# Turns and lag products of the state-space tiles earlier in layer 1's head periods, and their powers from coefficient tables

## What is computed

```python
def s5_mixer(u, lam_re, lam_im, log_step, b_re, b_im, c_re, c_im, d_skip, w_glu, b_glu):
    ...
    mag = jnp.exp(lr * dt)
    ab_r = mag * jnp.cos(li * dt)
    ab_i = mag * jnp.sin(li * dt)
    ...
    bb_r = fr[..., None] * br - fi[..., None] * bi
    bb_i = fr[..., None] * bi + fi[..., None] * br
    ...
    _, _, s_r, s_i = lax.associative_scan(_complex_linear_combine, (a_r, a_i, bu_r, bu_i), axis=1)
    y = (jnp.einsum('blgp,gcp->blgc', s_r, c_re.astype(f32))
         - jnp.einsum('blgp,gcp->blgc', s_i, c_im.astype(f32))
         + d_skip.astype(f32).reshape(SSM_GROUPS, SSM_GROUP) * ug)
```

## Time and profile before

| | us |
|---|---|
| median of 3 runs | 2592.64 (2587.49 to 2593.14) |
| the profiled execution | 2586.36 |
| its span | 2584.7 |
| layer 1's tiles on PE, first to last | 552.7 to 1022.4 |
| mean granted clock of PE over the span | 0.985 |
| busy: PE, DVE, ACT, POOL | 96%, 65%, 47%, 24% |

### The profile page before, as it was taken

How to read it: one execution, slowest core, us unless ns; L and a number is a source line. 1 busy time by engine, 2 the same in 40 slices (tenths; PEclk the granted TensorE clock), 3 DMA queues, 4 the chain that set the end, 5 groups by cost and what they waited for, 6 DMA issues and landing times.

```text
span 2584.7 us, 50520 instructions
## 1 busy us (share of the span) xinstructions
PE 2476.3 (96%) x18072; PEld 2348.0 (91%) x18072; DVE 1691.9 (65%) x2556; ACT 1220.9 (47%) x1819; POOL 628.6 (24%) x1047
## 2 busy tenths in 40 slices
PE   7999999989999999999988999999999999999999
PEld 7899999989899999998888999999888888888888
DVE  7876666567777777667777766565555555555555
ACT  5344544445555555555665434444544444444443
POOL 3300031358778886220010222011000000000000
PEclk9999999999999999999999999999999999999999
DMA  6655575555555555555454777565666676767764
GB/s 234 209 181 195 175 221 178 186 173 174 166 177 182 186 184 188 159 165 191 141 169 152 234 234 239 201 218 173 191 191 187 187 187 186 186 186 187 187 185 157
DMA packets 217449, 484.85 MB, mean 188 GB/s; under 512 B 22760, under 2 KB 120724, under 8 KB 217088
## 3 DMA queue, kind: packets, MB, share of 16 engines
q1 hardware_dynamic: 182912, 415.29, 52.6%
q0 software_dynamic: 13216, 37.93, 4.7%
q10 hardware_dynamic: 21216, 30.22, 3.6%
HBM read 455.00 MB, written 31.08 MB: 188 GB/s over the span
## 4 chain that ended last, share of the span: by engine, by line
PE 69%; DVE 15%; issue 7%; ACT 5%; POOL 2%; ACTq 1%; DVEq 0%; DMA 0%; POOLq 0%
PE z_ps L1987 12%; PE z_ps L1988 12%; PE z_ps L1989 12%; PE z_ps L2323 6%; PE z_ps L2324 6%; PE z_ps L2329 6%; DVE w_lo L1297 5%; ACT w_hi L717 2%; PE o_ps L2358 1%; PE o_ps L2357 1%; PE o_ps L2356 1%; PE v_ps L2357 1%; PE v_ps L2356 1%; PE p_ps L2357 1%; PE v_ps L2358 1%
## 5 line engine op out<-in xcount | busy, mean ns | idle before, releaser
L1297 DVE TENSOR_TENSOR w_lo<-w_raw,w_hi 128x1024 fp32r<-128x1024 f32 x520 | 634.8, 1249 | 335.4 <-ACT w_hi L717 333.1
L1987 PE MATMUL z_ps<-x_hi,w_hi 128*128 128x256 f32 x2816 | 822.1, 292 | 16.9 <-DVE w_lo L1290 14.4
L1988 PE MATMUL z_ps<-x_lo,w_hi 128*128 128x256 f32 x2816 | 805.3, 286 | 0.0
L1989 PE MATMUL z_ps<-x_hi,w_lo 128*128 128x256 f32 x2816 | 804.9, 286 | 0.0
L717 ACT ACTIVATE w_hi<-w_raw 128x1024 fp32r<-128x1024 f32 x520 | 533.1, 1051 | 262.5 <-PE z_ps L1989 216.5
L1987 PEld LDWEIGHTS z_ps<-x_hi,w_hi 128*128 128x128 f32 x2816 | 549.0, 195 | 26.9 <-issue 18.8
L1988 PEld LDWEIGHTS z_ps<-x_lo,w_hi 128*128 128x128 f32 x2816 | 549.3, 195 | 1.0
L1989 PEld LDWEIGHTS z_ps<-x_hi,w_lo 128*128 128x128 f32 x2816 | 548.9, 195 | 0.0
L1877 DVE TENSOR_TENSOR w_lo<-w_raw,w_hi 128x1024 fp32r<-128x1024 f32 x262 | 320.8, 1225 | 314.8 <-ACT w_hi L1141 314.7
L1141 ACT ACTIVATE w_hi<-w_raw 128x1024 fp32r<-128x1024 f32 x262 | 277.7, 1060 | 427.9 <-PE z_ps L2329 272.5
L2323 PE MATMUL z_ps<-w_hi,x_hi 128*128 128x512 f32 x704 | 275.1, 391 | 0.6 <-DVE res L1853 0.6
(11 more groups left out here) (382 smaller groups left out, 4131.5 us busy)
## 6 DMA issues: line engine op xcount, KB each, us to landing
w_raw<-in_w SPq DMA_DIRECT2D x704, 512.0 KB, 4.3
w_raw<-in_w SPq DMA_DIRECT2D x80, 384.0 KB, 4.8
res<-tab_d POOLq DMA_DIRECT2D x32, 384.0 KB, 4.5
w_raw<-in_w SPq DMA_DIRECT2D x80, 128.0 KB, 2.9
tab_d<-arena ACTq DMA_DIRECT2D x32, 256.0 KB, 2.1
tab_d<-arena POOLq DMA_DIRECT2D x32, 128.0 KB, 3.4
sg_d<-arena ACTq DMA_DIRECT2D x32, 128.0 KB, 4.6
arena<-sg_d POOLq DMA_DIRECT2D x16, 256.0 KB, 3.8
```

What stands on the lines that cost most here:

```text
L1297: dve.tensor_tensor(w_lo[:, n % RING, :], w_raw[:, n % RING, :], w_hi[:, n % RING, :].bitcast(F32), ALU.subtract).then_inc(w_lo_ready, 1)
L1987: pe.matmul(z, wh, hi[:, kt, :], start=(first and i == 0), stop=False)
L1988: pe.matmul(z, wh, lo[:, kt, :], start=False, stop=False)
L1989: m = pe.matmul(z, wl, hi[:, kt, :], start=False, stop=(last and i == len(kts) - 1))
```

## The change

- DVE's `tile` is split into `tile_turns` and `tile_lags`. The even tile's turns move ahead of `split_lo(p, 2)`, its lags to behind `split_lo(p, 3)`, ahead of the softmax's scaling. The odd tile's turns take the place where the even tile was, ahead of `split_lo(p, 4)`; its lags stay at the period's end. In head 0, with its norm, the even lags stand behind `split_lo(p, 2)`, and ACT's part of tile 0 moves from behind `split_hi(p, 3)` to behind `split_hi(p, 2)`.
- PE's tile asks for `e_ready` and `m_ready` up to tile `st - 2` instead of `st - 1`. The askings ahead of job 1 and job 3 stay.
- POOL makes tables of coefficients once (`coefficients`, in layer 0): the factor times powers 0 to 4 for C, powers 1 to 3 for B, for all 32 tiles. A tile is then twelve tensor_tensor instructions with broadcast operands, six of 160 columns and six of 96, no power waiting for the one before. The C half comes first and no longer waits for B. `load_c` for the next tile is issued after seven of them. A packed copy of the step times is made too.
- DVE waits once, at the start of layer 1, for the tables.

```diff
+                c_re, c_im, b_re, b_im = over(c_in[:, 0, :], 5), over(c_in[:, 1, :], 5), over(x[:, 0, 8, :], 3), over(x[:, 1, 8, :], 3)
+                c_out, b_out = [x[:, r, 0:5, :] for r in range(2)], [x[:, r, 5:8, :] for r in range(2)]
+                pool.tensor_tensor(c_tmp, c_im, by(c_coef, 1, 5), ALU.mult).then_inc(xt_step, 1)
+                pool.tensor_tensor(c_out[0], c_re, by(c_coef, 0, 5), ALU.mult).then_inc(xt_step, 1)
+                pool.tensor_tensor(c_out[1], c_im, by(c_coef, 0, 5), ALU.mult).then_inc(xt_step, 1)
+                pool.wait_ge(xt_step, at + 2)
+                pool.tensor_tensor(c_out[0], c_out[0], c_tmp, ALU.subtract).then_inc(xt_step, 1)
+                pool.wait_ge(bt_ready, st + 1)
+                pool.tensor_tensor(b_tmp, b_im, by(b_coef, 1, 3), ALU.mult).then_inc(xt_step, 1)
...
+            pool.wait_ge(t_vec_landed, 16)
+            coefficients()
             load_c(0)
             with pool.Fori(0, KT // 2) as n:
                 sum_squares(0, n, False)
-            tile_powers(0)
+            tile_powers(0, nr)
...
+                if norm and l == 1:
+                    tile(0, 0)
                 if prev:
                     softmax_exp(g - 1, prev and not prev2)
...
-                if l == 1:
+                if l == 1 and not norm:
                     tile(2 * h, 0, last)
...
+                if l == 1:
+                    tile_turns(2 * h)
                 split_lo(p, 2)
+                if norm and l == 1:
+                    tile_lags(0, 0)
...
                 if not norm:
                     split_lo(p, 3)
+                    if l == 1:
+                        tile_lags(2 * h, 0, last)
                 if prev:
                     softmax_scale(g - 1)
...
                 if l == 1:
-                    tile(2 * h, 0, last)
+                    tile_turns(2 * h + 1)
                 split_lo(p, 4)
...
                 if l == 1:
-                    tile(2 * h + 1, 1, last)
+                    tile_lags(2 * h + 1, 1, last)
...
-                pe.wait_ge(xt_step, 15 * st + 15)
-                reach(pe, e_ready, st)
-                reach(pe, m_ready, st)
+                pe.wait_ge(xt_step, 21 + 12 * st + 12)
+                reach(pe, e_ready, st - 1)
+                reach(pe, m_ready, st - 1)
```

More of the change, by code:

```diff
@@ L126, in build @@
         top[1] = top[0]
-        rel_at = top[0]
+        t_vec = part(1, 1, row)
         cos_r, sin_r, rstd_m, msq = (part(1, 1, row) for _ in range(4))
-        rope_cos, rope_sin, sqf, msq_sum, t_vec = (part(1, 1, row) for _ in range(5))
+        rope_cos, rope_sin, sqf, msq_sum = (part(1, 1, row) for _ in range(4))
+        c_coef = arena[:, 6 * T:6 * T + 320].rearrange("p (r m s) -> p r m s", r=2, m=5)
+        b_coef = arena[:, 6 * T + 320:8 * T].rearrange("p (r m s) -> p r m s", r=2, m=3)
         tile_at = top[0]
@@ L543, in load_c, with coefficients, tile_powers @@
                 pool.dma_start(c_in, ap["ssm_c"][st]).then_inc(c_landed, 16)
-            XT_STEPS = 15
-            def tile_powers(st):
+            COEF_STEPS = 21
+            XT_STEPS = 12
+            def coefficients():
+                pool.tensor_scalar(times_in, t_vec.rearrange("p (k i) -> p k i", i=STEP)[:, :, 0], 1.0, None,
+                                   ALU.mult).then_inc(xt_step, 1)
+                pool.tensor_scalar(c_coef[:, :, 0, :], ssm_c[:, 0:2, :], 1.0, None, ALU.mult).then_inc(xt_step, 1)
+                pool.wait_ge(xt_step, 1)
+                pool.tensor_scalar(b_coef[:, :, 2, :], ssm_lam[:], 1.0, None, ALU.mult).then_inc(xt_step, 1)
+                pool.wait_ge(xt_step, 3)
+                at = 3
+                lam = [ssm_lam[:, r, :].unsqueeze(1).to_broadcast([P, 2, ST]) for r in range(2)]
+                powers = [(c_coef, m, m + 1) for m in range(4)] + [(b_coef, m, m - 1) for m in (2, 1)]
+                for table, m, to in powers:
+                    pool.tensor_tensor(coef_t, table[:, :, m, :], lam[1], ALU.mult).then_inc(xt_step, 1)
+                    pool.tensor_tensor(table[:, :, to, :], table[:, :, m, :], lam[0], ALU.mult).then_inc(xt_step, 1)
+                    pool.wait_ge(xt_step, at + 2)
+                    pool.tensor_tensor(table[:, 0, to, :], table[:, 0, to, :], coef_t[:, 1, :], ALU.subtract)
+                    pool.tensor_tensor(table[:, 1, to, :], table[:, 1, to, :], coef_t[:, 0, :], ALU.add).then_inc(xt_step, 1)
+                    at += 3
+                    pool.wait_ge(xt_step, at)
+            def tile_powers(st, tmp=sq):
                 e = st % 2
-                x, at = xt[e], XT_STEPS * st
-                f_r, f_i = ssm_c[:, 0, st:st + 1], ssm_c[:, 1, st:st + 1]
-                l_r, l_i = ssm_lam[:, 0, st:st + 1], ssm_lam[:, 1, st:st + 1]
+                c_tmp = tmp[:, 0:160].rearrange("p (m c) -> p m c", m=5)
+                b_tmp = tmp[:, 160:256].rearrange("p (m c) -> p m c", m=3)
+                x, at = xt[e], COEF_STEPS + XT_STEPS * st
                 pool.wait_ge(c_landed, 16 * (st + 1))
@@ L555, in tile_powers @@
                 reach(pool, f_stored[e], 16 * (st // 2))
[L557 to L565, removed]
@@ L567, in tile_powers, with over, by @@
-                times(x[:, :, 0, :], c_in, xt_t[:, :, 0, :], f_r, f_i, 0)
+                def over(v, n):
+                    return v.unsqueeze(1).to_broadcast([P, n, 32])
+                def by(table, r, n):
+                    return table[:, r, :, st].unsqueeze(2).to_broadcast([P, n, 32])
+                c_re, c_im, b_re, b_im = over(c_in[:, 0, :], 5), over(c_in[:, 1, :], 5), over(x[:, 0, 8, :], 3), over(x[:, 1, 8, :], 3)
+                c_out, b_out = [x[:, r, 0:5, :] for r in range(2)], [x[:, r, 5:8, :] for r in range(2)]
@@ L568, in tile_powers @@
+                pool.wait_ge(xt_step, at + 4)
+                pool.tensor_tensor(c_tmp, c_re, by(c_coef, 1, 5), ALU.mult).then_inc(xt_step, 1)
+                pool.tensor_tensor(b_out[0], b_re, by(b_coef, 0, 3), ALU.mult).then_inc(xt_step, 1)
+                pool.wait_ge(xt_step, at + 6)
                 if st + 1 < ST:
                     load_c(st + 1)
-                pool.wait_ge(bt_ready, st + 1)
-                for m in range(3):
-                    times(x[:, :, m + 1:8 - m:6 - 2 * m, :], x[:, :, m:9 - m:8 - 2 * m, :], xt_t, l_r, l_i, 3 + 3 * m)
@@ L573, in tile_powers @@
-                times(x[:, :, 4, :], x[:, :, 3, :], xt_t[:, :, 0, :], l_r, l_i, 12)
+                pool.tensor_tensor(c_out[1], c_out[1], c_tmp, ALU.add).then_inc(xt_step, 1)
+                pool.tensor_tensor(b_out[1], b_im, by(b_coef, 0, 3), ALU.mult).then_inc(xt_step, 1)
+                pool.wait_ge(xt_step, at + 7)
+                pool.tensor_tensor(b_out[0], b_out[0], b_tmp, ALU.subtract).then_inc(xt_step, 1)
+                pool.wait_ge(xt_step, at + 10)
+                pool.tensor_tensor(b_tmp, b_re, by(b_coef, 1, 3), ALU.mult).then_inc(xt_step, 1)
@@ L574, in tile_powers @@
                 pool.dma_start(tab_d[st][:, 4 * P:TAB].rearrange("p (r b c) -> p r b c", r=2, b=4),
                                x[:, :, 1:5, :]).then_inc(f_stored[e], 16)
+                pool.wait_ge(xt_step, at + 11)
+                pool.tensor_tensor(b_out[1], b_out[1], b_tmp, ALU.add).then_inc(xt_step, 1)
             for i in range(N_NA):
@@ L1386, in out_block, with tile_turns @@
                                          op1=ALU.subtract).then_inc(x_lo_ready, 1)
-            times_in = t_vec.rearrange("p (k i) -> p k i", i=STEP)[:, :, 0]
-            def tile(st, e, last=False):
-                k_ps = tile_bank(z_ps[3 - 2 * e])[1]
+            def tile_turns(st):
                 reach(dve, tab_ready, st)
@@ L1404, in tile, with tile_lags @@
                 dve.tensor_scalar(turns, turns, 0.5, -0.5, ALU.min, ALU.max).then_inc(turns_ready, 1)
+            def tile_lags(st, e, last=False):
+                k_ps = tile_bank(z_ps[3 - 2 * e])[1]
                 dve.wait_ge(e_ready, st + 1)
@@ L1482, in _ @@
                     dve.wait_ge(consts_landed, (7 + STEP) * 16)
+                    dve.wait_ge(xt_step, 21)
                     chain(dve.tensor_copy(d_col.rearrange("p (c s) -> p s c", s=SPC), d_in))
```

7 lines of the change are left out of this document (4 added, 3 removed).

## The result

The changed kernel takes 2565.93 us, median of 4 runs (2563.41 to 2570.70), against 2591.56 for the kernel before (2587.49 to 2593.14): a ratio of 0.9906, 95% interval 0.9887 to 0.9924. I had forecast 2557 and a range of 2546 to 2580. The sign and the range were right, a quarter of the gain is missing. The profiled execution took 2563.41, with a span of 2561.5.

The account below looks back on a forecast made before the run. PE was taken to wait at odd tiles for DVE's late lag product of the even tile, not POOL. Gains 20.7 + 1.9 + 8.1 + 1.7 = 32.4 us gave 2554 (profiled) or 2560 (median); forecast 2557, range 2546 to 2580.

Parts of the forecast that it names:

- The waits, 20.7 us: PE's waits at odd tiles, heads 1 to 15: 22.2 us go, less 1.5 us left in dilated heads.
- The margin of 0.2 us in dilated heads: Heads 1 to 5: k's result leaves its bank 0.2 us before PE comes to the odd tile.
- the first rival: Waits of about 1 us return at k's bank, DVE's chain late or held by POOL: 2576 us, chance 0.2.
- Head 0, 1.9 us: Wait at head 0's odd tile shortens, less ACT's later start there: gain 1.9 us, between 0 and 2.95.
- The clock, 8.1 us: Five even halves slowed by a low PE clock behind waits return to normal: gain 8.1 us, between 0 and 8.1.
- The layer's end, 1.7 us: PE's 4.69 us wait for the last `y_lo` shortens as ACT starts sooner: gain 1.7 us, between 0 and 1.8.
- the 10 to 11 forecast: A tile on POOL with the new instructions takes 10 to 11 us, disturbance, DMA issues and waits included.
- Up to 13.9 it gains or costs nothing: POOL's tile time does not matter while it stays within 13.9 us, half of a 27.8 us period.
- POOL's 3 us of disturbance by DVE: DVE's accesses add 3 us to POOL's old tile of 8.1 us; the same 3 taken for the new tile.
- The second: Rival: POOL's new instructions cost twice the estimate, every odd tile waits for POOL: 2614 us, chance 0.05.
- The third: Rival: the change does nothing, PE waiting for the powers themselves or POOL's C half no sooner: 2588 us, chance 0.04.
- The fourth, 2548: Rival: everything and a little more, the lags and head 0 at their best ends: 2548 us, chance 0.05.

Follow-up runs that it names:

- e1: The changed kernel with the 15 old dependent power steps per tile on POOL, tables made but not read: 2555.91 us, ratio 0.9858.
- e2: The kernel before plus only the coefficient tables and packed times; DVE, ACT and PE as before: 2615.71 us, ratio 1.0102.
- e3: The kernel before with only PE's two askings moved to one tile earlier, as in the changed kernel: 2589.81 us, ratio 0.9992.
- e11: The changed kernel, but in every second tile POOL's B side waits for the odd tile's turns: 2557.94 us, ratio 0.9863.
- e4: The changed kernel with PE's two askings for the last tile, as before the change: 2561.60 us, ratio 0.9886.
- e9: The changed kernel with even lags behind k's evacuation, head 0 reordered too, and the old powers on POOL: 2569.73 us, ratio 0.9916.
- e5: The changed kernel with the even tile's lags behind k's evacuation in all periods but head 0: 2564.87 us, ratio 0.9903.
- e8: The changed kernel with POOL's arithmetic of each tile done twice: 2594.33 us, ratio 1.0009.
- e10: The changed kernel, but each of POOL's 12 instructions of a tile waits for the one before it: 2563.45 us, ratio 0.9894.

## Why the prediction was right, and where it was not

**What bounds.** Right: the even tile's lags held the odd one, not POOL as the list said. e1 has the old powers and the new order, and all sixteen waits for the lags are gone; the order alone gains 36 us (e1), the tables alone lose 24 (e2), both together gain 26. e3 corrects the picture of the bound: it was a loop through ACT and DVE, in which moving PE alone gains nothing clear of the noise.

**The waits, 20.7 us.** The odd halves (even tile to odd tile) of heads 1 to 15 took 220.2 us and take 201.1: 19.1 gained, with waits of 4.0 left. e1, with waits of 1.9 left, gained 22.2; that is more than the forecast, since a half without a wait takes 13.05 us and not the 13.2 of the prediction. The margin of 0.2 us in dilated heads was the step at risk, as the first rival said, and by its mechanism: of the 0.95 us each, 0.35 (e11) to 0.5 (e1) go when POOL's new instructions do not run beside the scaling. The rest is in the main the chain's start, later than in head 1; why it is late was not tried.

**Head 0, 1.9 us.** Nothing after (21.28 against 21.15 us for its half); e1 gives 1.9. The difference is DVE held up again: in the changed kernel the tile's first turn (L1433) took 1.36 us and the pair of splits in front of the norm 3.36, in e1 0.36 and 2.49.

**The clock, 8.1 us.** All of it came: no half is longer than 15.0 us from head 1 on, where five were 16.05 to 16.75. The even halves (odd tile to the next even one) together are 8.3 us shorter. Nor is one of the waits of 0.9 to 1.0 us followed by a slow half.

**The layer's end, 1.7 us.** 4.69 became 3.0.

**POOL.** A tile costs it 7.2 us of instructions and 1.3 of DMA issues, less than the 10 to 11 forecast. Its instructions without disturbance, min/median/max ns:

```profile
L590 POOL TENSOR_TENSOR arena<-arena x27: 457/467/1547, 608.7 to 972.8; 128x160 f32<-128x160 f32 x27
```

```profile
L603 POOL TENSOR_TENSOR arena<-arena x27: 340/353/363, 614.2 to 977.6; 128x96 f32<-128x96 f32 x27
```

Forecast were 0.52 and 0.37. The rate is (467 - 353) / 64 = 1.8 ns a column. The rule of the Trainium skill's GPSIMD Engine Reference, section 7, that speaks against the distant coefficients does not show: the subtraction of 160 columns (L593), which reads none of them, has a median of 529 ns. Held behind DVE, single instructions of 160 columns took up to 1.55 us, over the 1 us that was to undo the change, and undid nothing. "Up to 13.9 it gains or costs nothing" is the step that failed. I added POOL's 3 us of disturbance by DVE to POOL's tile; what the same meeting does to DVE stands only in the first rival, and the sum has no term for it. e2 prices it at 23 us of the stage where the turns are on the path, e1 at 5.1 in the new order. Where the new instructions are left out, the sum of the stage, 20.7 + 1.9 + 8.1 = 30.7, stands against 32.4 in e1, and 2557 against e1's 2556. That the second pair is this close is luck in part: the forecast was set between 2554 and 2560.

The sum of 32.4 us stands against 25.6 by the medians. In the stage 27.3 of 30.7 came; the 3.4 that lack are within what e1 gives back, 5.1. With the layer's end that makes 29.0; the other 3.4 us lie outside. A part of them can be scatter: e4, with the same stage, has a median 4 us lower, and in e1 stage and layer's end, 34.1, come near its 35.7 by the medians. Whether layer 0, 3.5 us longer up to the first tile in the changed kernel's profile, is part of it I can't say: it varies by 5.5 between the profiles, with nearly the same code up to there.

**The rivals.** The first came true in part, in four heads instead of fifteen. The second holds for the old powers in another order (e9), not for the new. The third was excluded by e1: with the powers as they were the waits went. The fourth, 2548, did not come; the fastest kernel here, e1, has a median of 2556.

## What to carry to other kernels

When work on GpSimd is changed, price what VectorE loses beside it, instruction by instruction on VectorE's critical stretch, and not only whether GpSimd is done in time; then place GpSimd's burst with one wait where VectorE has slack (e11: 2 us of the stage). A wait that is taken from one engine comes back, in the main, if the chain runs through others (e3, e5): before moving a step, list everyone who waits for it, the stores in their queues too. An engine that is about to bind can still cause no wait: follow its lead over its consumer (in e1 38 us, 6.5 to 9.3, then 2 to 3, at last 1.2).

## What the runs showed of the hardware

Where the two engines meet, one stands while the other's instruction runs, and not one instruction only: a scaling takes 0.35 us alone and up to 0.93 beside L602's 0.58; the first turn of head 0 took 1.36 instead of 0.36 while three of GpSimd's ran; e8's split took 3.19 instead of 1.21 while six did. The Trainium skill, SBUF — State Buffer, section "Who interferes with whom", gives the rule: a VectorE instruction in a two-port mode, which the scaling can be, and one of GpSimd shut each other out whole, and the one issued first wins; a VectorE instruction with two inputs in SBUF, as the weight split has, meets one of GpSimd that reads SBUF in the same way. The rows here agree for both sides, GpSimd's 2.11 for 0.43 beside two splits in e9 included. That the one that waits comes next is not what e8's rows show: GpSimd's six went first, one behind the other.

What I had not expected is how unequal GpSimd's forms are: the 12 new instructions of a tile, all with two inputs, hold VectorE more than the 20 old ones, though those kept GpSimd busy for 12.5 us a tile, DMA issues included, against 8.5 now. VectorE's busy time in the stage went from 342.5 to 371.5 us in the old order (e2) and from 344.0 (e1) to 357.7 in the new one. Gaps between them (e10) don't help, 361.5. Which property of the new ones does it, their length or their operands, was not tried.
